# A hybrid conv/GLA/MoE step on one core: expert rows formed on chip from a three-part bf16 split, for 18 groups instead of six

## What is computed

```
h2     = rmsnorm(x, norm2_w) * (1 + sc2) + sh2          # 384 x 1024, f32
scores = sigmoid(h2 @ w_router)                         # 64 experts
idx    = top_k(scores + b_router, 8)                    # 8 experts per token
wts    = scores[idx] / sum(scores[idx]) * 2.5
y      = sum over chosen e of wts * (silu(h2 @ Wg[e]) * (h2 @ Wu[e])) @ Wd[e]
x      = x + g2 * (y + shared_expert(h2))
```

## Time and profile before

| | |
|---|---|
| median of 3 runs | 956.34 us (955.24 to 956.64) |
| profiled execution, its own time | 954.98 us |
| its span, first to last instruction | 953.3 us |
| PE / PEld busy | 911.8 us (96%) / 488.0 us (51%) |
| DVE / ACT / POOL busy | 424.9 (45%) / 188.0 (20%) / 94.9 us (10%) |
| chain that ended last | PE 86%, DMA 7%, DVE 2%, issue 2%, ACT 1% |
| moved by DMA | 322.04 MB, mean 338 GB/s |
| mean granted clock of PE | 0.994 |

### The profile page before, as it was taken

How to read it: one execution, slowest core, us unless ns; L and a number is a source line. 1 busy time by engine, 2 the same in 40 slices (tenths; PEclk the granted TensorE clock), 3 DMA queues, 4 the chain that set the end, 5 groups by cost and what they waited for, 6 DMA issues and landing times.

```text
span 953.3 us, 13253 instructions
## 1 busy us (share of the span) xinstructions
PE 911.8 (96%) x5001; PEld 488.0 (51%) x5001; DVE 424.9 (45%) x769; ACT 188.0 (20%) x309; POOL 94.9 (10%) x198
## 2 busy tenths in 40 slices
PE   5899999999999999999999999989999989899996
PEld 2455567676555687544444444434445454354532
DVE  4129966534762336463333333223233323323267
ACT  3150601212100013112212212111121211212121
POOL 2000000000000000202122111111111201111100
PEclk9999999999999999999999999999999999999999
DMA  9998463625686356799999999999999999999996
GB/s 343 356 403 332 133 206 140 227 89 177 237 293 268 124 249 235 280 400 370 422 418 421 421 419 420 419 421 420 420 421 419 420 423 418 423 420 421 417 416 252
DMA packets 85034, 322.04 MB, mean 338 GB/s; under 512 B 10084, under 2 KB 38936, under 8 KB 56040
## 3 DMA queue, kind: packets, MB, share of 16 engines
q1 hardware_dynamic: 70368, 289.43, 76.4%
q0 software_dynamic: 9216, 22.22, 6.0%
q10 hardware_dynamic: 5384, 9.51, 2.7%
HBM read 298.36 MB, written 34.11 MB: 349 GB/s over the span
## 4 chain that ended last, share of the span: by engine, by line
PE 86%; DMA 7%; DVE 2%; issue 2%; ACT 1%; SPq 1%; DVEq 0%; POOLq 0%
PE bank L624 25%; PE bank L1910 21%; PE bank L653 13%; PE bank L2096 4%; PE bank L2082 4%; PE bank L610 3%; DMA arena<-expert_rows 3%; DMA arena<-in_w_mod_dram 3%; PE bank L2002 2%; PE bank L2124 2%; PE bank L604 2%; PE bank L577 2%; PE bank L642 1%; ACT arena L635 1%; DVE arena L638 1%
## 5 line engine op out<-in xcount | busy, mean ns | idle before, releaser
L624 PE MATMUL bank<-arena 128*32 128x512 f32 (+2 forms) x1568 | 258.4, 600 | 8.0 <-issue 8.0
L1910 PE MATMUL bank<-arena 128*128 128x384 f32 x640 | 209.9, 487 | 2.4 <-ACT arena L1697 2.4
L624 PEld LDWEIGHTS bank<-arena 128*32 128x32 f32 (+2 forms) x1568 | 90.2, 124 | 171.3 <-issue 171.1
L1910 PEld LDWEIGHTS bank<-arena 128*128 128x128 f32 x640 | 120.3, 190 | 85.6 <-issue 5.2
L653 PE MATMUL bank<-arena 128*32 128x512 f32 (+2 forms) x784 | 131.5, 596 | 4.9 <-issue 4.2
L653 PEld LDWEIGHTS bank<-arena 128*32 128x32 f32 (+2 forms) x784 | 43.1, 122 | 69.8 <-issue 69.1
L658 DVE SCALAR_TENSOR_TENSOR arena<-bank,arena 128x512 f32<-128x512 f32 x36 | 27.0, 751 | 106.5 <-PE bank L653 106.3
L666 ACT ACTIVATE arena<-arena 128x1024 f32<-128x1024 f32 x36 | 41.3, 1148 | 163.1 <-DVE arena L662 159.3
L463 DVE SCALAR_TENSOR_TENSOR arena<-arena 128x2048 f32<-128x2048 f32 x28 | 64.6, 2348 | 18.5 <-DMA arena<-in_w_mod_dram 17.4
L638 DVE TENSOR_TENSOR arena<-arena,bank 128x256 f32<-128x256 f32 x36 | 21.9, 607 | 85.7 <-ACT arena L635 85.7
L570 DVE TENSOR_TENSOR arena<-arena 128x288 f32<-128x288 f32 (+3 forms) x64 | 22.0, 380 | 82.2 <-POOL arena L741 41.2
(11 more groups left out here) (262 smaller groups left out, 796.1 us busy)
## 6 DMA issues: line engine op xcount, KB each, us to landing
arena<-in_w_up_e_dram SPq DMA_DIRECT2D x64, 1024.0 KB, 29.3
arena<-in_w_down_e_dram SPq DMA_DIRECT2D x64, 1024.0 KB, 29.2
arena<-in_w_gate_e_dram SPq DMA_DIRECT2D x64, 1024.0 KB, 27.3
arena<-in_w_mod_dram SPq DMA_DIRECT2D x24, 1024.0 KB, 7.4
arena<-in_w_in_dram SPq DMA_DIRECT2D x22, 1024.0 KB, 7.7
expert_rows<-arena SPq DMA_DIRECT2D x6, 2048.0 KB, 22.1
arena<-expert_rows SPq DMA_DIRECT2D x12, 1024.0 KB, 21.8
arena<-in_w_out_dram SPq DMA_DIRECT2D x4, 1024.0 KB, 5.3
```

What stands on the lines that cost most here:

```text
L624: ins = pe.matmul(bank[off:off + width, :], x_T[:, k, off:off + width], w[:, :, k, :], start=(k == 0), stop=(k == KT - 1))
L1910: ins = pe.matmul(ps[:, 0:TOK], w[:, k, P * (n % 2):P * (n % 2) + P], hT[:, k, :], start=(k == 0), stop=(k == KT - 1))
```

## The change

The normalised rows are split into three bf16 arrays, `high`, `middle` and `lowest`, whose sum is the f32 value. ACT writes `high` during pass 0 (once the copy of `h2` is in DRAM), DVE takes it off `h2` in pass 1, ACT writes `middle` in pass 2, DVE subtracts it in pass 3 and writes `lowest` over `h2`. Each of these is one instruction over 128 x 3072. PE waits for all four before it first forms rows on chip.

`ON_CHIP` grows to 18 groups: 7, 9, 11, 12, 13, 15, 17, 19, 20, 21, 23, 25, 27, 28, 29, 31, 33, 34. Forming a half now takes 4 blocks x 3 token tiles x 3 parts = 36 bf16 matmuls of 128 x 128 with 128 columns.

The one-hot tables become bf16. So do the numbers multiplied with them: the token number and the destination row are given as sums of parts that bf16 holds, the weight in three parts; a constant row is added by one more matmul per table, and the product has eight columns. `row_numbers` sums the parts with two reductions. The places are kept apart in f32 (`place_of`, `qplace`), so POOL's `pick` makes two copies for each expert instead of one, and `values` has seven instructions at its end instead of three. The arrays take 3072 more words per partition, and the scratch for DMAs issued by POOL is set to 4096 bytes. Five step semaphores become one counter, and two constants' semaphores are joined with a third.

```diff
-FAR = 8192.0
+FAR = 4096.0
-ON_CHIP = [15, 19, 23, 27, 31, 34]
+ON_CHIP = sorted([*range(7, 34, 2), 12, 20, 28, 34])
-        SIZE = 53200
+        SIZE = 53200 + 3072
+        high, middle = [at(take(NT * D // 2), NT * D // 2).bitcast(BF16).rearrange("p (t d) -> p t d", t=NT)
+                        for n in range(2)]
+        lowest = h2.rearrange("p t d -> p (t d)").bitcast(BF16).rearrange("p (t d) -> p t d", t=NT)[:, :, 0:D]
         def pick(pool, b, s, e):
-            return pool.tensor_copy(qv[:, b % 2, s], vals[:, :, bass.ds(e, 1), :].rearrange("p t e v -> p t (e v)"))
+            pool.tensor_copy(qv[:, b % 2, s, :, 3:7], traits[:, :, bass.ds(e, 1), :].rearrange("p t e v -> p t (e v)"))
+            return pool.tensor_copy(qplace[:, b % 2, s, :], place_of[:, :, bass.ds(e, 1)].rearrange("p t e -> p (t e)"))
         def table(pe, b, s, off, width):
             for o, w in [(32, 32), (64, 64)] if (off, width) == (32, 96) else [(off, width)]:
+                pe.matmul(banks[7][o:o + w, 0:8], ones_half[:, o:o + w], far, start=True, stop=False)
                 for t in range(NT):
-                    ins = pe.matmul(banks[7][o:o + w, 0:4], onehot[b][:, t, o:o + w], qv[:, b % 2, s, t, :],
-                                    start=(t == 0), stop=(t == NT - 1))
+                    ins = pe.matmul(banks[7][o:o + w, 0:8], onehot[b][:, t, o:o + w], qv[:, b % 2, s, t, :],
+                                    start=False, stop=(t == NT - 1))
-        def row_numbers(dve, b):
-            dve.tensor_tensor(rows_i[:, b, :], banks[7][:, 1:3], far, ALU.add)
...
+        def row_numbers(dve, x, b, times):
+            dve.tensor_reduce(row_sums, banks[7][:, 0:4].rearrange("p (j v) -> p v j", v=2), AX.X, ALU.add)                .then_inc(x["summed"], 1)
...
+            dve.tensor_reduce(wt[:, b:b + 1], banks[7][:, 4:7], AX.X, ALU.add)
+            dve.wait_ge(x["summed"], times)
+            return dve.tensor_copy(rows_i[:, b, :], row_sums)
         def rows_from_tokens(pe, b, part):
             for k in part:
                 for t in range(NT):
-                    ins = pe.matmul(banks[k // 4][:, P * (k % 4):P * (k % 4) + P], h2[:, t, P * k:P * k + P],
-                                    onehot[b][:, t, :], start=(t == 0), stop=(t == NT - 1))
+                    for n, rows in enumerate((high, middle, lowest)):
+                        ins = pe.matmul(banks[k // 4][:, P * (k % 4):P * (k % 4) + P], rows[:, t, P * k:P * k + P],
+                                        onehot[b][:, t, :], start=(t == 0 and n == 0), stop=(t == NT - 1 and n == 2))
             return ins
                 if i in ON_CHIP:
+                    pe.wait_ge(S["split_done"], 4)
                     pe.wait_ge(x["onehot_done"], i + 1)
# act_experts, behind the second half of the features of group i + 1
+                if i == 0:
+                    act.wait_ge(S["h2_out"], 16 * NT)
+                if i in (0, 2):
+                    act.wait_ge(S["split_done"], i)
+                    act.activation((high, middle)[i // 2], h2, ACT.Copy).then_inc(S["split_done"], 1)
                 if i == 0:
                     act.wait_ge(S["tile_folded"], 1)
                     begin_gate(0)
# dve_loop, behind the first half of the features of group i + 1
+                if i in (1, 3):
+                    dve.wait_ge(S["split_done"], i)
+                    dve.tensor_tensor((h2, lowest)[i // 2], h2, (high, middle)[i // 2], ALU.subtract)\
+                        .then_inc(S["split_done"], 1)
# values(t)
-                dve.tensor_scalar(vals[:, t, :, 1], ones[:, 0:NE], tok_far[:, 0, one], None, ALU.mult)
-                dve.tensor_scalar(vals[:, t, :, 2], rank[:, t, :], tok_far[:, 1, one], None, ALU.add)
-                link(dve.tensor_scalar(vals[:, t, :, 3], scores[:, t, :], weight_sum[:, one], ROUTED_SCALE,
+                dve.tensor_scalar(traits[:, t, :, 0], rank[:, t, :], low, None, ALU.add)
+                link(dve.tensor_scalar(scores[:, t, :], scores[:, t, :], weight_sum[:, one], ROUTED_SCALE,
                                        ALU.mult, ALU.mult))
+                for part in (1, 2):
+                    link(dve.tensor_copy(traits[:, t, :, part], scores[:, t, :]))
+                    link(dve.tensor_tensor(scores[:, t, :], scores[:, t, :], traits[:, t, :, part], ALU.subtract))
+                link(dve.tensor_copy(traits[:, t, :, 3], scores[:, t, :]))
-    nc = _bacc.Bacc("TRN2", target_bir_lowering=False, num_devices=1)
+    nc = _bacc.Bacc("TRN2", target_bir_lowering=False, num_devices=1, dynamic_dma_scratch_size=4096)
```

More of the change, by code:

```diff
@@ L316, in program, with row_table @@
         mod_rows = at(a_rows, 3, 512)
-        vals = at(a_rows, NT, NE, 4)
-        onehot = [at(a, NT, ROWS) for a in (a_rows + 768, a_rows + 768 + NT * ROWS)]
-        places = [at(a, TOK) for a in (a_rows + 768, a_rows + 768 + NT * ROWS)]
+        place_of = at(a_rows, NT, NE)
+        traits = at(a_rows + NT * NE, 2 * NT * NE).bitcast(BF16).rearrange("p (t e v) -> p t e v", t=NT, v=4)
+        a_hot = a_rows + 3 * NT * NE
+        def row_table(a):
+            return at(a, NT * ROWS // 2).bitcast(BF16).rearrange("p (t r) -> p t r", t=NT)
+        onehot = [row_table(a) for a in (a_hot + NT * ROWS, a_hot + 3 * NT * ROWS // 2)]
+        places = [at(a, TOK) for a in (a_hot, a_hot + NT * ROWS)]
+        qplace = at(a_hot + 2 * NT * ROWS, 2, 2, NT)
+        assert a_hot + 2 * NT * ROWS + 4 * NT <= a_rows + 1536
         a_z = take(512)
@@ L357, in program @@
         part_f = at(take(1), 1)
-        far = at(take(2), 2)
+        far = at(take(4), 4).bitcast(BF16)
+        row_sums = at(take(2), 2)
+        low = at(take(1), 1)
+        low_i = at(take(1), 1).bitcast(I32)
         most_f = at(take(1), 1)
         most_i = at(take(1), 1).bitcast(I32)
-        tok_far = at(take(2 * NT), 2, NT)
+        static = at(take(2 * NT), 2, NT)
         of_seq = at(take(8), 2, 4)
@@ L453, in unit_arrived, with step @@
             eng.wait_ge(unit_in[n % UNITS], 16 * (n // UNITS + 1))
+        def step(eng, name):
+            eng.wait_ge(S["step_done"], STEPS.index(name) + 1)
         def add_modulation(eng, g, k, link):
@@ L571, in mark @@
+        def mark(dve, table, b, s, off, width):
+            return dve.tensor_tensor(table[:, :, off:off + width],
                                      deal[width].unsqueeze(1).to_broadcast([P, NT, width]),
-                                     qv[:, b % 2, s, :, 0:1].to_broadcast([P, NT, width]), ALU.is_equal)
+                                     qplace[:, b % 2, s, :].unsqueeze(2).to_broadcast([P, NT, width]), ALU.is_equal)
         def table(pe, b, s, off, width):
             for o, w in [(32, 32), (64, 64)] if (off, width) == (32, 96) else [(off, width)]:
+                pe.matmul(banks[7][o:o + w, 0:8], ones_half[:, o:o + w], far, start=True, stop=False)
@@ L895, in one_hot @@
                 for s, (rank, off, width) in enumerate(QUADS[i]):
-                    ins = mark(dve, i % 2, s, off, width)
+                    ins = mark(dve, onehot[i % 2], i, s, off, width)
                 ins.then_inc(x["onehot_done"], 1)
@@ L1102, in vector_part_a @@
             link(dve.tensor_copy(iota1, iota_i))
-            link(dve.memset(far[:, 0:1], FAR))
-            link(dve.memset(far[:, 1:2], TOPK * FAR))
+            link(dve.memset(far, 0.0))
+            dve.memset(far[0:1, 0:2], FAR)
+            link(dve.tensor_single_scalar(low_i, part_i, 3, ALU.bitwise_and))
+            link(dve.tensor_copy(low, low_i))
+            link(dve.tensor_scalar(low, low, float(TOPK), None, ALU.mult))
             for t in range(NT):
-                dve.tensor_scalar(tok_far[:, 0, t:t + 1], part_f, float(P * t) - FAR, None, ALU.add)
-                link(dve.tensor_scalar(tok_far[:, 1, t:t + 1], part_f, float(P * t) - FAR, float(TOPK), ALU.add, ALU.mult))
+                dve.memset(static[:, 0, t:t + 1], P * t - FAR)
+                link(dve.scalar_tensor_tensor(out=static[:, 1, t:t + 1], in0=part_f, scalar=float(TOPK), in1=low,
+                                              op0=ALU.mult, op1=ALU.subtract))
+                link(dve.tensor_scalar(static[:, 1, t:t + 1], static[:, 1, t:t + 1], TOPK * P * t - FAR, None, ALU.add))
             job = ("cols",)
@@ L1401, in vector_part_a @@
                 link(dve.tensor_scalar(key_col[0:n, :], key_col[0:n, :], -PRIOR, None, ALU.add))
+            for b in range(2):
+                for s in range(2):
+                    dve.tensor_copy(qv[:, b, s, :, 0:2], static.rearrange("p v t -> p t v"))
+                    dve.tensor_copy(qv[:, b, s, :, 2:3], part_f.unsqueeze(1).to_broadcast([P, NT, 1]))
+                    link(dve.memset(qv[:, b, s, :, 7:8], 0.0))
             dve.wait_ge(S["router_in"], 32)
@@ L1742, in _ @@
                     act.activation(f[:, d], f[:, d], ACT.Exp, scale=1.0 / GATE_NORM).then_inc(S["exp_ready"], 1)
-            act.wait_ge(S["conv_done"], 1)
+            step(act, "conv_done")
```

(6 more changed lines are left out.)

59 lines of the change are left out of this document (29 added, 30 removed).

## The result

The changed kernel takes 957.52 us (median of 20 runs) against 955.74 for the kernel before on the same chips: a ratio of 1.0017, 95% interval 1.0010 to 1.0024. It is slower, by 1.8 us, where +5.8 had been forecast. The interval leaves out 1, so the direction holds; but 1.8 us is under the 0.2% that the prediction itself called no change, and a third of the forecast, and that is what has to be explained.

What follows compares the result with a forecast made beforehand. It took PE's own chain and the transfers, within about 2% of each other, as bounds; -11.5 + 16.4 - 0.8 + 1.2 + 1.2 - 0.7 = +5.8 us gave 962.1 us against the median 956.34, range 952 to 972.

Steps and rivals of the forecast that it cites:

- The first rival: Whole loop: the transfers alone decide, so it ends 10.7 us earlier, at 945.6 us; chance 0.12.
- the fourth: Expert loop: weight loads refill the freed transfer time and PE's stops remain, 973.6 us; chance 0.05.
- The third: Forming halves: weight loads set the step, 112 ns giving 1033 us; decides from some 60 ns on; chance 0.05.
- ahead of the loop: Before the first product: extra DVE steps and POOL copies delay one-hot, tables and first gather, +1.2 us.
- the split in passes 0 to 3: Early passes: ACT's 3.4 us copy delays group 0's weighting and what follows, so PE waits +1.2 us.
- stops and slow products: PE in the loop: waits for weights and the slow products behind them all go, -11.5 us.
- forming on chip: PE in 18 passes: halves of 2.05 us, surplus 2.27 each, less six old surpluses of 4.09, +16.4 us.
- tables in gathered passes: Gathered passes where the table ends last: shorter tables save 0.15 us in each of five, -0.8 us.
- the end: Reading rows back after the loop: fewer weight loads still under way, -0.7 us.
- what the transfers gain: Expert loop: twelve gathers go, 0.89 us each, 10.7 in all; every PE stop for weights goes, -11.5 us.
- The second rival: Whole kernel about even: small terms at their good ends and a 50 ns forming step, 955 us; chance 0.18.

Runs made afterwards that it cites:

- The run with six groups: Changed kernel with only the old six groups (15, 19, 23, 27, 31, 34) formed on chip, in bf16: 956.91 us, ratio to before 1.0017.
- the run with one part: Changed kernel, 18 groups, with the middle and lowest parts left out of the products that form rows, giving bf16 accuracy only: 946.30 us, ratio 0.9900.
- eighteen in f32: Kernel before with the change's longer list of 18 groups formed on chip, in f32 as before: 988.95 us, ratio 1.0351.
- after: The changed kernel itself, 18 groups formed on chip in three bf16 parts, against the kernel before: 957.52 us, ratio 1.0017.
- The run with the later split: Changed kernel with fourteen groups, the split one pass later, and DVE instead of PE adding the last piece's first row: 951.31 us, ratio 0.9959.
- fourteen groups: Changed kernel with fourteen groups (7, 9, ... 33) formed on chip instead of 18: 949.73 us, ratio 0.9938.

## Why the prediction was right or wrong

**Right: the picture.** Two limits close together, stops that go when transfers are relieved, and PE paying for the rest. The run with six groups (PE's work cut, no time won) and the run with one part (946) show the transfers' limit; eighteen in f32 and eighteen in bf16 show PE's. The first rival, transfers alone, is refuted by after itself; the fourth by the missing stops. The third, weight loads that set a step of 60 ns or more, is refuted by the 56 ns step. These are the 1296 matmuls and loads of the halves (busy us, mean ns of one):

```profile
L634 PE MATMUL bank<-arena 128*128 128x128 bf16 x1296 | 78.3, 219 | 0.0
```
```profile
L634 PEld LDWEIGHTS bank<-arena 128*128 128x128 bf16 x1296 | 73.9, 98 | 0.5
```

A load takes 98 ns, but 1296 of them are busy for 73.9 us only, 57 ns each, so loads overlap each other and 98 is not the step. Whether the loads or the columns set the 56 ns, no run here separates. The 81 ns that the Trainium skill's page "TensorE: Matmul & The Clock Gate", section "Back-to-back issue gap", gives for such a stream does not show here; the 56 ns that the same section gives for the isolated gap does.

**Wrong: the size.** The measured terms, from the starts of the products and the ends of the spans:

| step of the prediction | forecast | measured |
|---|---|---|
| ahead of the loop | +1.2 | +1.23 (406.48 - 405.25) |
| the split in passes 0 to 3 | +1.2 | +0.22 (pass 1; passes 2 and 3 as before) |
| stops and slow products | -11.5 | -12.1 |
| forming on chip | +16.4 | +14.1 |
| tables in gathered passes | -0.8 | -0.2 (pass 0 -0.16, the rest -0.03 together) |
| the end | -0.7 | -1.35 (45.11 - 46.46) |
| sum | +5.8 | +1.9 |

The forecast was a small difference between a term of about -12 and one of about +16. Forming is off by 2.3 us and the split by 1.0, the stops and the end by some 0.6 each, all four the same way; the tables, off by 0.6 the other way, hid a part of it. Together they make 3.9 us, two thirds of the forecast. The step that failed first is **"forming on chip, 18 times"**. Its halves were right (2.05 forecast, 2.01 to 2.12 measured), and so was the mechanism; what it had wrong is the surplus. That was 17.04 less 12.95, a pass with 64 + 64 rows from the chain less one with 96 + 32 rows. By the starts of products, without stops and slow products, the six old passes take 16.95 on average, the twelve that were gathered before 13.04, and the 18 formed after 15.13, not 15.22. So the twelve new ones cost 25.5 us (12 x 2.12, for 12 x 2.27), and the six old ones give back 11.4 (6 x 1.90, for 6 x 1.82): 14.1. The table, which I took as 0.30 in all of them, is 0.19 with rows as in group 23's pass and some 0.45 with 96 + 32 rows.

The saving in **"tables in gathered passes"** did not come: the table is shorter, but what ends last there is the leg over ACT and DVE, so PE only waits longer for the silu product (the 8.6 us for 3.4 above). Without stops and slow products these passes, but for pass 0, take what they took before.

Second, **"the split in passes 0 to 3"**. ACT's copy of 128 x 3072 took 2.76 us, not 3.4; priced as three gate multiplications it was 0.6 too dear. Counted from the start of pass 1's product (428.40 before, 429.47 after), the weighting of group 0 slipped by 1.86 us and the one-hot behind POOL's picks by 2.10, so POOL's extra copies added 0.24, not 0.5. Of these 2.10 the silu product on DVE had 1.78 to spare, and 0.25 came through to PE in pass 1. The one-hot before, and the changed kernel's timeline:

```profile
432.60 0.63 DVE L570 TENSOR_TENSOR arena<-arena 128x288 f32<-128x288 f32 x2 [2.52 <-POOL arena L567]
```
```profile
426.37 2.76 ACT L913 ACTIVATE arena<-arena 128x3072 bf16<-128x3072 f32 x1
...
431.60 0.75 DVE L682 SCALAR_TENSOR_TENSOR arena<-bank,arena 128x512 f32<-128x512 f32 x1
...
435.77 0.63 DVE L590 TENSOR_TENSOR arena<-arena 128x288 bf16<-128x288 f32 x2 [2.76 <-POOL arena L587]
...
436.62 0.64 ACT L659 ACTIVATE arena<-bank 128x256 f32<-128x256 f32 x1 [2.38 <-PE bank L648]
...
437.51 0.59 DVE L662 TENSOR_TENSOR arena<-arena,bank 128x256 f32<-128x256 f32 x1
...
438.16 0.44 PE L666 MATMUL bank<-arena 128*128 128x128 f32 x2 [0.56 <-DVE arena L662]
```

The silu ends at 437.26 and the product starts at 437.51: 0.25, where the earlier trace rows have it start 0.03 behind. The run with the later split takes that quarter away.

Third, **"what the transfers gain"**: by the starts of products, the five passes of the kernel before with a stop or a slow product took 12.1 us more than passes of their kind, where the pieces of the chain in the earlier trace rows gave 11.5; the 0.6 between the two views is not explained. Fourth, **"the end"**: PE's adds of the pieces read back took 16.83 us before (from 928.38 to the end of the last row, 945.21) and now run unbroken in 15.61, so 1.2 of the 1.35 are gained there; I had counted only the 0.58 that the two bracketed waits show.

The second rival, small terms at their good ends, gave 955 as its time, and 957.5 lies nearer to it than to the forecast's 962.1. That is in part luck: of its terms the split and the end went that way, while the start and the tables did not, nor did its chief one, a step of 50 ns.

**Right: ahead of the loop.** The first table waited for its one-hot, and began 1.9 us later than in the earlier trace rows, where 1.8 had been worked out; the row of after:

```profile
393.31 0.18 PE L596 MATMUL bank<-arena 128*96 128x8 bf16 x1 [1.41 <-DVE arena L590]
...
406.48 7.07 PE L648 MATMUL bank<-arena 128*32 128x512 f32 x64
```

That the whole term agrees to 0.03 is partly luck: in the runs with the same code up to there the first product starts at 406.49 to 407.33, a spread that arises ahead of the routing.

## What to carry to other kernels

Where two limits lie within 2% of each other, find what one step of the knob does to each (here +2.0 us on PE's chain, -0.88 us on the transfers) and set it where they meet: fourteen groups are 0.6% faster than six in f32, and eighteen are slower than both. A forecast that is the difference of two terms of 12 and 15 needs each to a few tenths: take a surplus between passes of the same shape and from the same view. A wait seen in one kernel says nothing of its neighbour with another setting; read it again before cutting it.

## What the runs showed that was not expected

A queue of transfers at 420 GB/s in nearly every slice does not say that it is the limit: it is as flat in the kernel with fourteen groups, which never stops for weights, as in the one with six, which stops for 16.5 us. What tells is the stop on the engine that is fed. And a stop costs more than itself: behind four of the seven in the run with six the next product took 8.48 to 8.80 us instead of 7.0. Two stretches of that run, before its first stop and from it on (PE, PEld, DVE, ACT, POOL busy, granted clock, DMA share, GB/s):

```profile
600.00:625.00 25.00, 24.11 (x264) 10.96 (x260) 8.48 (x22) 5.50 (x8) 5.46 (x12) 1.00 1.02 420
628.00:652.00 24.00, 20.61 (x133) 8.58 (x134) 7.36 (x17) 3.90 (x5) 4.61 (x13) 0.93 1.02 422
```

The slow product of the second stretch, in two pieces:

```profile
630.90:635.00 4.10, 4.10 (x24) 1.37 (x28) 1.82 (x3) 0.00 (x0) 0.45 (x3) 0.58 1.01 421
635.00:639.70 4.70, 4.70 (x49) 1.70 (x42) 0.00 (x0) 0.00 (x0) 0.00 (x0) 1.00 1.02 421
```

PE stood still for 3.61 us, and the clock granted in the stretch fell from 1.00 (2.4 GHz) to a mean of 0.93. All of the fall lies in the first 4.1 us of the product behind the stop: 0.58 there, so most of that ran at the lower level, 1.2 GHz, and 1.00 again behind it. At 0.58 these 4.1 us lose 4.1 x 0.42 = 1.7 us, about the 1.8 by which the product was too long. In my forecast this was the 3.50 us of slow products.
